# Borders of the feed-forward part: another order of operands, low parts, gate and last stores

## The reference

```python
mix = jnp.concatenate([o_a, o_b, o_c], axis=-1) @ w_out[l]
x = x + rmsnorm(mix, g_mix_post[l])
f = conv_glu_ffn(rmsnorm(x, g_ffn_pre[l]), w_up[l], conv_w[l], conv_b[l], w_down[l])
x = x + rmsnorm(f, g_ffn_post[l])

def conv_glu_ffn(h, w_up, conv_w, conv_b, w_down):
    u = h @ w_up                                   # 1024 -> 2 x 2816
    u = causal depthwise convolution of width 3 over the tokens, + conv_b
    a, b = jnp.split(u, 2, axis=-1)
    return (jax.nn.gelu(a, approximate=True) * b) @ w_down
```

## Time and profile before

| | us |
|---|---|
| median of 3 runs | 3173.92 |
| lowest and highest run | 3173.43, 3177.03 |
| span of the profiled execution, first to last instruction | 3174.1 |
| TensorE busy | 3066.0 (97%) |
| VectorE busy | 2058.5 (65%) |
| ScalarE busy | 1472.0 (46%) |
| GpSimd busy | 1211.7 (38%) |

### The profile page before, as it was taken

One profiled execution on the slowest core, in us unless ns is written; L12 is line 12 of the kernel. 1 busy time (PEld: TensorE's weight loads), 2 busy tenths in 40 slices (PEclk: granted clock), 3 DMA queues, 4 the chain that ended last, 5 costly groups with the idle time before them and its releaser, 6 DMA issues. The chain is left out here.

```text
span 3174.1 us, 44910 instructions
## 1 busy us (share of the span) xinstructions
PE 3066.0 (97%) x16138; PEld 2501.5 (79%) x16138; DVE 2058.5 (65%) x3930; ACT 1472.0 (46%) x2657; POOL 1211.7 (38%) x845
## 2 busy tenths in 40 slices
PE   8999999998998999999989989999999999999998
PEld 8888888887776776666668878888888788888887
DVE  5565566556767987777744587777645577777443
ACT  5332533236666866665633444444434344444332
POOL 2444254310000024442110098888210698885010
PEclk9999999998999999999999999999999999999999
DMA  4465555378778743332234522222565222223553
GB/s 141 161 186 149 169 162 174 114 209 195 183 187 215 175 114 73 96 99 50 84 93 132 162 99 80 87 80 80 175 200 201 102 85 80 93 80 110 182 199 106
DMA packets 262540, 425.58 MB, mean 134 GB/s; under 512 B 126801, under 2 KB 162897, under 8 KB 250321
## 3 DMA queue, kind: packets, MB, share of 16 engines
q1 hardware_dynamic: 252752, 385.28, 41.4%
q0 software_dynamic: 9568, 37.43, 3.7%
HBM read 304.19 MB, written 126.84 MB: 136 GB/s over the span
## 5 line engine op out<-in xcount | busy, mean ns | idle before, releaser
L1080 PE MATMUL z_banks<-ops,z_area 128*128 128x512 f32 x1720 | 434.1, 391 | 3.2 <-DVE z_area L834 3.2
L3153 PE MATMUL f_banks<-f_wt 128*128 128x512 f32 x1776 | 406.1, 389 | 0.0
L3153 PEld LDWEIGHTS f_banks<-f_wt 128*128 128x128 f32 x1776 | 333.3, 188 | 69.2
L1080 PEld LDWEIGHTS z_banks<-ops,z_area 128*128 128x128 f32 x1720 | 323.0, 188 | 70.4 <-DVE z_area L834 3.6
L2540 POOL TENSOR_TENSOR f_wt<-f_wt_f,f_wt 128x1024 fp32r<-128x1024 f32 x132 | 320.2, 2449 | 60.3 <-ACT f_wt L2668 59.4
L2022 ACT ACTIVATE w_small<-w_small,a_stats 128x128 f32<-128x128 f32 (+3 forms) x510 | 257.3, 517 | 110.7 <-DVE a_stats L2108 82.6
L3124 PE MATMUL f_banks<-low,f_wt 128*128 128x512 f32 x704 | 275.3, 391 | 0.0
L2108 DVE CUSTOM_DVE_ANT_0 w_small<-a_s_ps,near 128x128 f32<-128x128 f32 (+2 forms) x456 | 166.2, 392 | 110.1 <-PE a_s_ps L1908 86.8
L2949 DVE SCALAR_TENSOR_TENSOR near<-w_small,vk,near 128x1024 f32<-128x1024 f32 x88 | 232.3, 2640 | 1.7
L3124 PE MATMUL f_banks<-f_oo,f_wt 128*128 128x512 f32 x704 | 218.0, 391 | 3.2 <-issue 3.0
L1952 PE MATMUL a_ot_ps<-a_turned_w,vs 128*64 128x256 f32 (+3 forms) x1452 | 220.9, 427 | 0.0
(11 more groups left out here) (305 smaller groups left out, 7120.4 us busy)
## 6 DMA issues: line engine op xcount, KB each, us to landing
f_wt_f<-in_w_ffn SPq DMA_DIRECT2D x74, 512.0 KB, 4.1
z_area_f<-in_w_z SPq DMA_DIRECT2D x54, 512.0 KB, 5.1
low<-z_hi SPq DMA_DIRECT2D x48, 512.0 KB, 7.9
f_raw_f<-in_w_ffn SPq DMA_DIRECT2D x22, 1024.0 KB, 4.8
f_wt_f<-in_w_ffn SPq DMA_DIRECT2D x22, 1024.0 KB, 5.3
g_up<-near SPq DMA_DIRECT2D x44, 512.0 KB, 2.6
f_wt_f<-g_up SPq DMA_DIRECT2D x88, 256.0 KB, 4.4
low<-z_lo SPq DMA_DIRECT2D x39, 512.0 KB, 8.6
```

The source lines that it names most:

```text
L1080: last = pe.matmul(banks[:, bank, :], w[:, c * P:(c + 1) * P], rows[:, c * 512:(c + 1) * 512], start=(first and c == 0 and q == 0), stop=( ...
L3153: last = pe.matmul(banks[:, 2 * t + n, :], g[:, tok], w[:, n, :], start=(d == 0 and x == 0), stop=(d == NF - 1 and x == 2))
```

## The change

The pairing of products with their needs and the split order: T1 comes third and B21 fourth. In the first round of all, the first low part (A11, A12) is formed by VectorE (`first_lower`), and GpSimd waits for it after its fourth sum. The gate of round n-1 moves behind the P7 and the P5 sum, in every round. The last two stores of the first half (tiles 6 and 7) are issued by SyncE instead of GpSimd, with semaphores of their own. ScalarE's orders at both borders change to fit.

```diff
-PRODUCTS = ((0, A11, B11, True, 1, 1), (1, S2, T2, True, 2, 2), (0, A12, B21, False, 1, 3), (2, S3, T3, True, 3, 5),
-            (3, S1, T1, True, 3, 4), (2, A22, T4, False, 4, 6), (3, S4, B22, False, 4, 7))
-SPLIT_ORDER = (B11, T2, B21, T1, T3, T4, B22)
+PRODUCTS = ((0, A11, B11, True, 1, 1), (1, S2, T2, True, 2, 2), (0, A12, B21, False, 1, 4), (2, S3, T3, True, 3, 5),
+            (3, S1, T1, True, 3, 3), (2, A22, T4, False, 4, 6), (3, S4, B22, False, 4, 7))
+SPLIT_ORDER = (B11, T2, T1, B21, T3, T4, B22)
...
@@ SyncE, start of the second half
                     load_raw(n0 + 2)
+                    for t in range(2 * TILES - 2, 2 * TILES):
+                        sp.wait_ge(out_done, t + 1)
+                        sp.dma_start(out[t * P:(t + 1) * P, :], x2[t % TILES]).then_inc(middle_out[t % 2], 16)
@@ GpSimd, form(n)
                 sums_a(n)
-                lower_a(n, A11, 2, raw[:, 0:2], 1)
+                if n:
+                    lower_a(n, A11, 2, raw[:, 0:2], 1)
                 sum_b(n)
+                if n == 0:
+                    pool.wait_ge(al_done, 1)
...
                         lower_a(NF, A22, 1, raw[:, 3:4], 2)
-                        for t in range(t0 + 2, t0 + TILES):
-                            store(t)
                         continue
@@ ScalarE, projection tiles
                     take_o(t + 1)
+                else:
+                    upper_b(0, 2)
...
                     upper_a22(0)
+                    upper_b(0, 3)
                     upper_s12(0)
-                    upper_b(0, 2)
-                    upper_b(0, 3)
                     upper_s34(0)
@@ ScalarE, rounds
+                    elif n == NF:
+                        take_c11(n)
+                        upper_a22(n + 1)
+                        for i in range(2):
+                            act.wait_ge(stored[2 + i], 16)
+                            act.wait_ge(middle_out[i], 16)
+                        upper_b(1, 6)
+                        upper_s12(n + 1)
                     else:
                         upper_a22(n + 1)
                         upper_s12(n + 1)
-                    take_c11(n)
-                    if n == NF:
-                        for i in (2, 3):
-                            act.wait_ge(stored[i], 32)
-                        upper_b(1, 6)
+                    if n != NF:
+                        take_c11(n)
@@ VectorE
+            def first_lower():
+                dve.wait_ge(ah_done, 1)
+                dve.tensor_tensor(a_lo(0, A11, 2), raws[0][:, 0:2], a_hi(0, A11, 2).bitcast(F32), ALU.subtract)\
+                   .then_inc(al_done, 1)
...
                     take_o(t + 1)
+                else:
+                    lower_b(0, 2)
...
                 if t == NT - 1:
-                    lower_b(0, 2)
+                    first_lower()
                     lower_b(0, 3)
...
                     add_p6(n)
-                    if n > n0:
-                        gate(n - 1)
...
                     add_p5(n)
+                    if n > n0:
+                        gate(n - 1)
```

More of the change, by code:

```diff
@@ L2378, in mix_ffn @@
         stored = [sem(f"stored{i}") for i in range(TILES)]
+        middle_out = [sem("middle_out0"), sem("middle_out1")]
         last_stored = sem("last_stored")
@@ L2617, in _ @@
                     for t in range(t0, t0 + TILES):
-                        pool.wait_ge(stored[t % TILES], 16 * (q + 1))
+                        pool.wait_ge(stored[t % TILES], 16 * (q + 1 if t % TILES < 2 or q == 0 else q))
                         load_x(t + TILES)
             for i in range(TILES):
-                pool.wait_ge(stored[i], 16 * (NT // TILES - 1))
+                pool.wait_ge(stored[i], 16 * (NT // TILES - 1 if i < 2 else NT // TILES - 2))
         @blk.scalar
```

## The result

The changed kernel takes 3196.36 us (median of 4 runs, 3194.09 to 3198.73) against 3173.68 before; the ratio is 1.0069, with a 95% interval of 1.0055 to 1.0084: 22.7 us slower. The forecast was 3184.

What follows compares the result with a forecast made beforehand. TensorE, busy 97%, was taken as the bound, with gaps at the borders and VectorE and GpSimd turns nearly full. 3174.1 - 2.1 - 5.0 - 3.4 + 20 = 3183.6, about 3184; own range 3176 to 3200, 8-in-10 range 3162 to 3208.

Steps and rivals of the forecast that it cites:

- First border: Start of the first half: T3 ready earlier and P7 sum no longer behind the gate; forecast -7.1 us.
- The two terms: Start of the first half: T3's earlier low part gains 2.1 us, the later gate at round 1 gains 5.0 us.
- the 1.0 us of the later first product: Round 0: VectorE's low part behind GpSimd's S4 puts the first product at 1825.6 instead of 1824.6.
- Settled rounds: Rounds 2 to 20 of each half: the later gate delays C21; TensorE waits 1.1 us every second round, +20 us.
- a tie: Second settled round: gate and S1/S2 low part both ask at 2043.9; forecast let the gate get in first.
- Second border: Start of the second half: SyncE stores and earlier GpSimd sums start the seventh product at 2518.8, not 2521.20; -3.4 us.
- VectorE's third residual sum end at 2508.15 as today: Start of the second half: this sum assumed not delayed by GpSimd's earlier sums; part of the -3.4 us.
- The third rival: Start of the second half: VectorE passed over until GpSimd pauses; +6.4 us, total 3190; within the 0.56, a quarter of 0.24.
- 38 x 1.8: Settled rounds: upper bound if GpSimd wins each tie, 1.8 us a round over 38 rounds, given as 69 us.
- Only the borders count: First rival: the late C21 in settled rounds does not reach TensorE; 3163.6 us, faster; chance 0.24.
- GpSimd first at every tie: Second rival: gate waits behind the S1/S2 low part in each settled round; 3233 us; chance 0.12 with mixtures.
- Gain and loss cancel: Fourth rival: ties fall so that only some ten settled rounds stall; 3174 us; chance 0.08.

Runs made afterwards that it cites:

- old-order kernel: The changed kernel with the gate between P7 and P5 sums and B21 before T1 again, first low part still by VectorE; 3172.79 us (ratio 0.9996).

## Why the prediction was right, and where its sizes were off

*First border: -7.1 forecast, -7.1 measured.* Moved by the 2.3 us of the unchanged part, the first product starts at 1825.6 (forecast 1825.6), T3's low part ends at 1836.7 (1836.6), P4 waits 1.03 us (1.0), P6 of round 0 0.79 (1.1), and P6 of round 1 does not wait. The two terms fit as well: the gate alone gives -5.2 (forecast -5.0), and the rest, from 54.5 to 52.7, gives -1.9 (forecast -2.1). One attribution was wrong: the step had the low part by VectorE lose the 1.0 us of the later first product. The old-order kernel shows that it gains 1.2 us there (5.9 against 7.2 us before), and that the new order costs 2.2.

*Settled rounds: slower, by the mechanism forecast.* The edge copy behind GpSimd's turn, C21 late, ScalarE's copy late, a wait of 1.1 us of the third product in every second round, the gate waiting in one round (2.98) and just first in the next (by 0.04 us): all are in the rows; the C21 sum is late by 3.1 and 1.3 us, where 2.9 and 1.4 were forecast; and the edge copy's part is shown by taking it away. That the gate wins in the second round was taken from a tie, and no row of before settled it; the right branch there is luck in part. In the profile after, from 1960 us on, the gate leads in every such round but one, by 0.02 to 0.07 us. In the one where it comes 0.05 us behind the pair (2545.21 against 2545.16) it takes 3.44 us, and the longest of the waits, 1.60 us, follows.

The size was off: 20 us forecast, 26.9 measured (11.9 and 15.0). The number of waits was nearly right (18 forecast, 20 measured); what each costs was not. A wait shown with 1.15 us costs 1.42: two rounds take 39.50 us, not 39.2, since the idle time is counted from the end of the last matmul (0.39 us long, but the next normally starts 0.23 after it), and the first pairs after it are some 0.1 us longer. 15 times 1.42 is 21.3; the five other waits, 4.2 us as shown, made their rounds 5.5 us longer.

*Second border: -3.4 forecast, +2.2 measured.* The step that failed is "VectorE's third residual sum end at 2508.15 as today". The third rival, passed over until S4 of round 23 is done, came true in its mechanism, at +2.2 where it gave +3.0 (6.4 more than -3.4). That the sizes are so near is luck in part: it put the wait before P7, but 7.92 us came before P6, for the P7 sum behind the residual sums, and P7 waited 0.69. This border makes 5.6 us of the 12.6 between the forecast change (+9.5) and the four stages (+22.1); the settled rounds' size is another 6.9. (Two slips of the working change nothing: with P7 2.4 us earlier its gap would be 3.5 us, not 3.0, and 38 x 1.8 is 68, not 69.)

*Rivals.* "Only the borders count" is refuted for this kernel, and is what the gate between P7 and P5 brings: 3168, where 3163.6 was given for it with a better second border. "GpSimd first at every tie" would be a stall in each of 38 rounds and is refuted by the 15 that come in every second one. "Gain and loss cancel", with some ten rounds stalled, is refuted by 20.

## What to carry to other kernels

Where two engines take turns, add up the turns of both against the period before moving a step of either: at 18.4 of 19.04 us the place of one 1.2 us gate was worth 27 us, because the gate left a hole in the neighbour's work and the two-column copy behind it had to wait for a whole turn. Move a step only past the sum that it holds up (here P7, not P5 too). And when a transfer moves to another queue, look at what stands ahead of it there.

## What the runs showed of the hardware

A VectorE sum that takes 1.22 us when nothing holds it off took 5.4 and 12.7 us beside an unbroken row of two and of seven GpSimd operations that followed two DMA issues; without DMA issues ahead of the row it took 3.0 us and the two engines took turns. One more thing differed: the sum started while GpSimd was issuing the stores (2505.25, within 2504.76 to 2505.93) in the one case, and 0.48 us into a subtraction in the other. Starting ahead of GpSimd is not enough by itself: the gate at 2039.00 was 0.04 us ahead and took 1.22. So the runs point to the DMA issue as the cause; how it does so stays open. The rule of the Trainium skill, page "SBUF — State Buffer", section "SBUF: two separate sides", that the pair is held for one instruction, fits the case of 3.0 us and not the other two.

The first product of round 0 came after the same waits (0.66 or 0.67 us, then 1.13) in the profile after and in the kernel with the gate between P7 and P5. It ran slow in the one (1.05 us a pair; granted clock 0.54 of full from 1823.25 to 1827.00, so mostly at 1.2 GHz) and at full clock, 2.4 GHz, in the other (0.73 us; 1.00 from 1820.78 to 1823.90). Of the nine profiles with the new order it ran slow in four, although what stands ahead of it is the same code in most of them; what decides is not shown.

```profile
1823.25 0.98 PE L3142 MATMUL f_banks<-vs,f_wt 128*128 128x512 f32 x2 [1.13 <-DVE f_wt L2907]
1824.45 1.05 PE L3142 MATMUL f_banks<-vs,f_wt 128*128 128x512 f32 x2
```
```profile
1820.78 0.73 PE L3142 MATMUL f_banks<-vs,f_wt 128*128 128x512 f32 x2 [1.13 <-DVE f_wt L2907]
```

It cost nothing there: with full clock, the second product waits 1.40 us for the low part of S1 and S2 and starts as far behind the first (4.43 us against 4.45).
